# A gated-delta-rule and HGRN2 mixer on one core: the triangular solve in four quadrants of TensorE, the recurrence in 32x32 squares, and new orders

## The reference

```python
# gated delta rule, chunks of c rows
a = jnp.where(strict, jnp.einsum('bhntd,bhnsd->bhnts', kb, k) * decay, 0.0)
t_inv = lax.linalg.triangular_solve(a + eye, eye, left_side=True, lower=True, unit_diagonal=True)
u = jnp.einsum('bhnts,bhnsv->bhntv', t_inv, v * beta[..., None])
# HGRN2: S_t = diag(f_t) S_{t-1} + k_t i_t^T, o_t = S_t^T q_t
dec = jnp.exp(jnp.where(incl, b_n[:, :, :, None, :] - b_n[:, :, None, :, :], -jnp.inf))
att = jnp.einsum('bhtd,bhsd,bhtsd->bhts', q_n, k_n, dec)
# gates
merged = (jax.nn.sigmoid(gate_dn) * (o_dn @ w_branch_dn) + jax.nn.sigmoid(gate_hg) * (o_hg @ w_branch_hg))
return merged @ w_out
```

## Time and profile before

| | us |
|---|---|
| median of 3 runs | 1531.16 (1530.28 to 1531.87) |
| the profiled execution | 1531.69 |
| its span | 1529.9 |
| TensorE busy | 1505.9 |
| VectorE busy | 1203.9 |
| ScalarE busy | 1015.9 |

### The profile page before, as it was taken

One profiled execution on the slowest core, in us unless ns is written; L12 is line 12 of the kernel. 1 busy time (PEld: TensorE's weight loads), 2 busy tenths in 40 slices (PEclk: granted clock), 3 DMA queues, 4 the chain that ended last, 5 costly groups with the idle time before them and its releaser, 6 DMA issues.

```text
span 1529.9 us, 29802 instructions
## 1 busy us (share of the span) xinstructions
PE 1505.9 (98%) x12684; PEld 1400.1 (92%) x12684; DVE 1203.9 (79%) x1702; ACT 1015.9 (66%) x1566; POOL 8.3 (1%) x18
## 2 busy tenths in 40 slices
PE   9999999999999999999999999999999998999998
PEld 9999999988889999999988889969999897899997
DVE  7999766889758799667898768876898578688864
ACT  7786865667646776765676546685777467677753
POOL 0000000000000000000000000000000001000000
PEclk9999999999999999999999999999999999999999
DMA  7522135555554422244655546402555543255551
GB/s 291 193 95 102 57 138 193 205 183 193 207 178 158 158 98 85 84 165 166 233 191 184 214 170 241 165 1 87 218 193 193 191 142 136 84 208 182 191 193 55
DMA packets 35700, 245.55 MB, mean 161 GB/s; under 512 B 4208, under 2 KB 4592, under 8 KB 6512
## 3 DMA queue, kind: packets, MB, share of 16 engines
q1 hardware_dynamic: 35568, 243.65, 44.5%
HBM read 242.58 MB, written 1.05 MB: 159 GB/s over the span
## 4 chain that ended last, share of the span: by engine, by line
PE 81%; DVE 11%; ACT 5%; DMA 1%; issue 1%; SPq 0%; DVEq 0%; ACTq 0%
PE PS L420 81%; DVE WL L1982 2%; DVE SB L1991 1%; DVE SB L1982 1%; DVE SA L1982 1%; ACT SB L1232 1%; DMA RAW<-w_in 1%; ACT WH L1235 1%; ACT SB L1909 1%; DVE SB L2260 1%; DVE SB L1986 1%; ACT SB L1235 1%; PE PS L423 0%; DVE SA L1991 0%; DVE SA L2162 0%
## 5 line engine op out<-in xcount | busy, mean ns | idle before, releaser
L420 PE MATMUL PS<-XHL,WH 128*128 128x256 f32 (+2 forms) x4080 | 847.9, 301 | 4.6 <-ACT SA L1410 2.8
L420 PEld LDWEIGHTS PS<-XHL,WH 128*128 128x128 f32 (+1 forms) x4080 | 645.8, 187 | 41.4 <-issue 5.9
L420 PE MATMUL PS<-XHL,WL 128*128 128x256 f32 (+1 forms) x2392 | 670.0, 280 | 0.0
L1235 ACT CAST WH<-RAW 128x2048 fp32r<-128x2048 f32 (+1 forms) x235 | 427.3, 1822 | 267.3 <-PE PS L420 255.4
L1982 DVE TENSOR_TENSOR WL<-RAW,WH 128x2048 fp32r<-128x2048 f32 (+1 forms) x235 | 512.0, 2181 | 109.2 <-ACT WH L1235 108.8
L420 PEld LDWEIGHTS PS<-XHL,WL 128*128 128x128 f32 (+1 forms) x2392 | 448.8, 188 | 0.4
L420 PE MATMUL PS<-INHL,WH 128*128 128x512 f32 (+1 forms) x1216 | 334.2, 343 | 0.0
L420 PE MATMUL PS<-INHL,WL 128*128 128x256 f32 x960 | 270.0, 281 | 0.0
L420 PEld LDWEIGHTS PS<-INHL,WH 128*128 128x128 f32 x1216 | 210.1, 188 | 27.6
L420 PEld LDWEIGHTS PS<-INHL,WL 128*128 128x128 f32 x960 | 181.2, 189 | 0.0
L1982 DVE TENSOR_TENSOR SB<-SB 128x510 f32<-128x510 f32 (+3 forms) x171 | 112.6, 660 | 14.8 <-ACT SB L1232 11.4
(11 more groups left out here) (156 smaller groups left out, 1436.7 us busy)
## 6 DMA issues: line engine op xcount, KB each, us to landing
RAW<-w_in SPq DMA_DIRECT2D x51, 1024.0 KB, 4.8
RAW<-w_up SPq DMA_DIRECT2D x44, 1024.0 KB, 4.8
RAW<-f_in SPq DMA_DIRECT2D x44, 1024.0 KB, 4.8
RAW<-w_down SPq DMA_DIRECT2D x22, 1024.0 KB, 4.8
RAW<-f_out SPq DMA_DIRECT2D x22, 1024.0 KB, 4.8
RAW<-a_w_in SPq DMA_DIRECT2D x10, 1024.0 KB, 4.9
RAW<-w_out SPq DMA_DIRECT2D x8, 1024.0 KB, 4.7
RAW<-w_bdn SPq DMA_DIRECT2D x4, 1024.0 KB, 4.8
```

The costliest lines, as they stand in the source:

```text
L420: return e.matmul(out, l, r, start=start, stop=stop, skip_group_check=True)
L1235: e.copy(out, x).then_inc(*A.up(*key, of=of))
```

## The change

1. In the solve, both directions go in lockstep: `dn_y(lv)` and `dn_z(lv)` issue 32 matmuls, for each unit two of direction 1 and two of direction 0, into two banks. Direction 0's y is written to the other half (`turned_half`), its `XT` is stored with halves swapped, so that direction 0 uses the other two quadrants. Its `back` becomes two transposes of 64 partitions.
2. dn_z of side 1 is gone: VectorE turns the corners of level 5 itself (`back5`). The side-1 copies on ScalarE go with it.
3. hg_diag and levels 0 to 4 use 32x32 squares: 32 matmuls of 32 columns by 32 in place of 16 of 64 by 64; `kept` and the diagonal's copy work on 256 columns instead of 512. Four copies instead of two bring them to `att`.
4. The gates' sums live in a buffer of their own (`GT`, 2048 columns) and in SB; `sqo` moves.
5. New orders on all three engines: a projection half stands between every two steps of the solve; hg(1) to hg(7) and o_hg move behind or between the gates; z_silu, tanh and the merging are placed anew, with eight table loads in a mixer instead of four; `ident_in` and `it_out(0)` go ahead of `dm_exp(3, .)`.

```diff
                 def dn_y(lv):
+                    p = [bank(st, "y", d, lv) for d in range(2)]
+                    for d in (1, 0):
+                        w.wait_ge(*V["pair", st, 3, d])
+                        side_placed(d, lv - 1, 0)
                     for m in range(8):
-                        for h in HALF:
-                            last = mm(p[h, m * 64:m * 64 + 64], at_d(d, 1 - m // 4)[h, m % 4, h], XIv[h, d, m], True, True)
+                        for d in (1, 0):
+                            for b, h in enumerate(HALF):
+                                last = mm(p[d][turned_half(d, b), m * 64:m * 64 + 64], at_d(d, 1 - m // 4)[h, m % 4, h], XIv[h, d, m], True, True)
...
                 def dn_z(lv):
-                            x, y = XTv[h, d, m], YBv[d][h, m]
-                            last = mm(p[h, m * 64:m * 64 + 64], *((x, y) if side == 0 else (y, x)), True, True)
+                                t = turned_half(d, b)
+                                last = mm(p[d][h, m * 64:m * 64 + 64], XTv[t, d, m], YBv[d][t, m], True, True)
...
+                        if lv < 5:
+                            for q in QUART:
+                                last = mm(p[q, m * 32:m * 32 + 32], zk[:, h, s, q], zq[:, h, s, q], True, True)
+                            continue
...
                 def back(d, lv):
+                    w.wait_ge(*V["placed", st, d, lv, 0])
                     x = slice(d * 512, d * 512 + 512)
-                    blocks_turned(XTc[:, x], XIc[:, x], "placed", st, d, lv, 1)
+                    if d:
+                        blocks_turned(XTc[:, x], XIc[:, x], "placed", st, d, lv, 1)
+                        return
+                    for b in range(2):
+                        blocks_turned(XTc[HALF[1 - b], x], XIc[HALF[b], x], "placed", st, d, lv, 1)
+                def back5(d):
+                    w.wait_ge(*A["placed", st, d, 5, 0])
+                    for b in range(2):
+                        blocks_turned(corner(XTv[:, d], b if d else 1 - b, 1 - d), corner(XIv[:, d], b, d), "placed", st, d, 5, 1)
```

More of the change, by code:

```diff
@@ L289, in program @@
         HALF = (slice(0, 64), slice(64, 128))
+        QUART = [slice(32 * j, 32 * j + 32) for j in range(4)]
         att = SB[:, 11264:13312]
@@ L660, in dn_z @@
[L660 to L663, removed]
-                    for m in range(8):
-                        for h in HALF:
-                            x, y = XTv[h, d, m], YBv[d][h, m]
-                            last = mm(p[h, m * 64:m * 64 + 64], *((x, y) if side == 0 else (y, x)), True, True)
-                    last.then_inc(*P.up("ps", st, "z", d, lv, side))
-                    ps.give(st, "z", d, lv, side)
+                    w.wait_ge(*(A if (lv, side) == (5, 0) else V)["placed", st, d, lv, side])
@@ new lines, in dn_z @@
+                def dn_z(lv):
+                    p = [bank(st, "z", d, lv) for d in range(2)]
+                    for d in (1, 0):
+                        w.wait_ge(*A["y", st, d, lv])
+                        side_placed(d, lv - 1, 1)
+                    for m in range(8):
+                        for d in (1, 0):
+                            for b, h in enumerate(HALF):
+                                t = turned_half(d, b)
+                                last = mm(p[d][h, m * 64:m * 64 + 64], XTv[t, d, m], YBv[d][t, m], True, True)
+                    last.then_inc(*P.up("ps", st, "z", lv))
+                    for d in range(2):
+                        ps.give(st, "z", d, lv)
@@ L671, in dn_y6 @@
                 def dn_y6():
-                    p = bank(st, "y6")
+                    p = [bank(st, "y6", d) for d in range(2)]
                     for d in range(2):
@@ L821, in mixer @@
[L821 to L826, removed]
+                zproj(2, 1)
+                dn_y(2)
+                zproj(3, 0)
+                dn_z(2)
+                hg(0)
+                zproj(3, 1)
+                dn_y(3)
+                gate(0, 0)
+                dn_z(3)
+                gate(1, 0)
+                dn_y(4)
+                gate(0, 1)
+                dn_z(4)
@@ L2362, in mixer @@
-                dn_first_back(1)
-                z_in(3)
+                chunk()
                 w.wait_ge(*V["w lo", z_after[l]])
                 zproj(0)
-                dn_first(0)
-                hg_mul(1)
-                dn_first_back(0)
+                zproj(1)
+                placed(0, 1)
+                hg_mul(0)
+                placed(1, 1)
                 z_in(2)
-                ref_neg()
+                back(0, 1)
+                back(1, 1)
                 chunk()
-                placed(1, 1)
@@ L2387, in mixer @@
+                placed(0, 3)
+                placed(1, 3)
+                chunk()
+                back(0, 3)
+                back(1, 3)
                 hg_mul(2)
-                back(1, 3)
-                placed(0, 3)
-                back(0, 3)
                 placed(1, 4)
+                placed(0, 4)
                 back(1, 4)
+                back(0, 4)
+                hg_mul(1)
+                gate(0)
+                gate(1)
+                chunk()
+                z_in(4)
                 z_in(7)
@@ L2394, in mixer @@
                 kept(1)
-                placed(0, 4)
+                back5(0)
+                back5(1)
+                chunk()
+                z_in(8)
                 z_in(6)
+                z_in(9)
+                gate(2)
                 kept(2, after=1)
-                z_in(9)
                 hg_mul(3)
-                z_in(8)
-                hg_mul(4)
-                back(0, 4)
-                zproj(2)
-                z_in(11)
-                kept(3, after=2)
-                z_in(10)
+                chunk()
@@ L2407, in mixer @@
+                gate(3)
+                z_in(11)
+                z_in(10)
+                kept(3, after=2)
+                tm_in(0)
+                hg_mul(4)
+                tm_in(1)
+                hg_mul(5)
                 z_in(13)
                 z_in(12)
-                hg_mul(5)
-                hg_mul(6)
                 kept(4, after=3)
@@ L3059, in constants @@
     r, c = np.arange(128)[:, None], np.arange(512)[None, :]
+    quarter = [mk[q:q + 32, 2, 0:5, q:q + 32].copy() for q in range(0, 128, 32)]
     for kind in range(3):
```

449 lines of the change are left out of this document (221 added, 228 removed).

## The result

The changed kernel takes **1506.46 us** (median of four runs, 1505.4 to 1507.83), the kernel before 1531.45 beside it (1530.28 to 1531.87): a ratio of 0.9837, 95% interval 0.9825 to 0.9849, so 25.0 us less. The forecast was 1508. The profiled run of the changed kernel took 1507.83 (span 1506.0), the slowest of its four.

The account below looks back on a forecast made before the run. The prediction took TensorE's own stream, busy 98% of the span, as the bound. Its terms, -9.4 - 1.9 - 0.7 + 2.5 - 1.9 = -11.4 us a mixer, -22.8 for two, gave 1508 us, with an 8-in-10 range of 1502 to 1526.

Parts of the forecast that it names:

- What bounds it: TensorE's own stream, busy 98% of the span; at most 2.1 us of waiting to win per mixer.
- Four quadrants: y and z groups of levels 1 to 5: four tiles at 14.7 ns a record, -9.4 us a mixer.
- eight starts that fit into 59 ns: Four starts of loads and four of matmuls at 6 ns, taken as 52 ns, within one tile's 59 ns.
- The rival of rationed starts: Slower mean start rate, say 22 ns a record: -3.2 us a mixer, 1525; chance 0.12, shared with quadrants not overlapping.
- start-to-start floor of 25 ns: Rival: at 25 ns a record gain and loss cancel, -0.1 us a mixer, no change, 1531; chance 0.05.
- Level 5's second side: Two dn_z groups with side 1 replaced by four small VectorE transposes: -1.9 us a mixer.
- 32x32 squares: hg_diag and recurrence levels 0 to 4, six groups at 0.83 us each instead of 0.94: -0.7 us a mixer.
- Changes of tiling: Small groups standing singly between projection halves: 10 more excursions at 0.33, 6 fewer inner changes at 0.14, +2.5 us a mixer.
- Waits that go: TensorE's wait behind it_out(0) (L1410), -1.3, and two waits of 0.33 each, -0.6: together -1.9 us a mixer.
- The two of 0.33: Waits in groups that a projection half of 2.8 us now precedes: -0.6 us a mixer.
- New waits: Waits in the solve's levels, costed at 0; as rival 1 us in each of five levels, 1518, chance 0.15.
- The margin of 0.5 us at y(1): VectorE's transposes ready at 122.6 us, TensorE coming to y(1) at 123.1, so no wait.

Follow-up runs that it names:

- two-quadrant kernel: The changed kernel with direction 0 put back into the same two diagonal 64x64 quadrants as direction 1: 1523.18 us, ratio 0.9945.
- the same edit: Identity copy and it_out(0) ahead of the four exponentials: put back behind them in the changed kernel, 1507.97 us; moved ahead in the kernel before, 1536.65 us.
- it_out(0) late: The changed kernel with ScalarE's identity copy and it_out(0) back behind the four exponentials of dm_exp(3, .): 1507.97 us, ratio 0.9841.
- two column tiles at a time: The changed kernel with each group of 32x32 squares doing the first two column tiles, then the other two: 1510.42 us, ratio 0.9856.
- diagonal pairs: The changed kernel with all matmuls of direction 1 first within a step, then all of direction 0: 1521.83 us, ratio 0.9932.
- shared rows: The changed kernel with a step first doing the two quadrants that read the same 64 rows, then the other two: 1519.6 us, ratio 0.9918.
- two runs that differ only in level 5: The changed kernel with level 5 of the recurrence also in 32x32 squares, 1504.81 us, and the unaltered changed kernel beside it, 1505.44 us.

## Why the prediction was right, point by point

The stretch from it(1) to the branch is 13.0 us shorter in the first mixer (from 123.18 to 110.14, counted from the start of the last projection) and 12.5 in the second (452.86 between the two mixers' branches before, 440.33 after). Together that is 25.6, and the medians gained 25.0. The prediction had 11.4 a mixer. The forecast is right for its reasons in the main; one term was mis-sized, and one margin was gone.

- **What bounds it.** A clean sum of TensorE's stream for the time: right. TensorE's busy time fell by 22.3 us, all of it in the two mixers, and its idle time there by 2.0 in the first and 1.3 in the second (2.09 to 0.77).
- **Four quadrants**, -9.4: the two-quadrant kernel gives 9.3 in the first mixer and (680.42 - 662.19) - (231.85 - 221.86) = 8.2 in the second, where the changed kernel has its stand of 0.57 us and this one has none. The price of 59 ns a tile and the independence of four tiles, each read from rows that showed one kind of overlap alone, were right. The reason that was given for four at once, eight starts that fit into 59 ns, was not needed: the squares show that such starts don't add up. (Eight starts at the 6 ns it names are 48 ns, not 52.) The rival of rationed starts falls by the step of 1.16 us, and so does that of the start-to-start floor of 25 ns that the Trainium skill gives ("TensorE: Matmul & The Clock Gate", section Wait — 56ns, not 53.3ns?): the mean here is 14.9.
- **Level 5's second side**, -1.9: the trace has 1408 records of 64*64 where it had 1536, 128 fewer, 64 a mixer. Their price then was 29.3 ns. No run puts this side back, so the term is counted and not measured.
- **32x32 squares**, -0.7, the **mis-sized term**: -2.3 measured. I took 0.83 us a group, from 52 ns of eight starts for each four records; it took 0.57. Starts of loads and of matmuls evidently don't add up: four tiles with eight starts go round in 32 ns. The value taken was the wrong one between the bounds; the lower bound, 32 ns for four records and 0.51 a group, has the beat that the records keep. The first mixer's surplus of 13.0 over 11.4 is this term.
- **Changes of tiling**, +2.5: in the trace an excursion costs again 0.21 - 0.12 = 0.09 on entry (150.58 to 150.79), then 0.14 and 0.11 on leaving, 0.34. This is the price of single places in the trace; no run takes one away alone.
- **Waits that go**, -1.9: the gap behind it(1) is 0.37 instead of 1.69, so -1.3; putting it back costs 1.1 net, since y(1) then stops waiting. The two of 0.33 are gone from the groups.
- **New waits**, 0: nearly. The margin of 0.5 us at y(1) was wrong: VectorE's transposes end at 123.48 (I had 122.6), while TensorE could have started at 123.45 (I had 123.1). It stands for 0.17 us, +0.2. That VectorE's 0.9 us cost no more is partly luck, as TensorE was late too. The later levels of the first mixer have no wait. The second mixer has one short stand of another kind, below.

With the quadrants and squares as measured, the waits as read, and level 5 and the changes of tiling as predicted, the sum is -9.3 - 1.9 - 2.3 + 2.5 - 1.9 + 0.2 = -12.7 for a measured -13.0. The stages behind the mixers are not part of the sum: from the second mixer's branch to the end they take 842.31 us in the profiled run before and 843.81 in that of after, and between 840.7 and 842.6 in the other kernels, whatever was edited in the mixers. The profiled run of after happened to be long there, so its span alone understates the gain.

## What to carry to other kernels

Price small matmuls by the tile, not by the array: find in the records how long one tile takes for one of them, and count how many tiles have work at a time; independent chains, such as the two directions of a recurrence, can share a step if each has its own quadrant. When a wait is removed by reordering an engine's work, look at who gets the delay: the same edit gained 1.5 us in the medians (1.1 in the first mixer's trace) where other work stood ahead of the next consumer, and lost some 5 where less did. Where a dependent pair of steps has no work between, look behind the wait too: the granted clock can fall there and cost nearly as much again.

## What the runs showed of the hardware

- Four 64*64 quadrants run fully side by side: 14.9 ns a record on the whole against 59 ns a tile, and for two tiles at a time it makes no difference whether they share rows, columns or neither (1.91 us for 64 records each).
- A 32-column record holds its tile for 32 ns, a 64-column record for 59. A group of 64 on four column tiles of 128*32 takes 8.9 ns a record on the whole.
- At a change from one set of tiles to another TensorE reaches ahead by about three records of a tile, 0.17 us at 64 columns (14 records instead of 8 in flight) and 0.1 us at 32.
- Stands of 2.38 and 2.64 us were followed by 4.00 and 6.29 us at a mean clock of 0.57 and 0.51, stands of 1.19 and 1.53 us in the same run by none. Stands of 2.72 and 2.80 us in another kernel were followed by full clock.
- **Open:** behind a group of 32x32 squares in the second mixer TensorE stood once for a time in which it waited for nothing that the profile shows. The timeline of the changed kernel:

```profile
603.81 0.68 PE L434 MATMUL PS<-SA 128*32 128x32 f32 x56
604.41 0.50 PE L434 MATMUL PS<-XHL,WH 128*128 128x256 f32 x2
605.49 0.38 PE L434 MATMUL PS<-XHL,WL 128*128 128x256 f32 x1 [0.57 <-issue]
```

Such stands came and went between kernels: 0.90 and 0.35 us in the one with it_out(0) late, 0.23 with two column tiles at a time, 0.29 behind the first record of a group of squares in the kernels of diagonal pairs and of shared rows, none in the two-quadrant kernel and in that with 64x64 squares, 0.72 and none in two runs that differ only in level 5. Bursts of short records use up instructions faster than projections do, so the supply of instructions is a candidate, but no run tested it.
